# A two-block network in f32: no throwaway passes, decay steps spread over more blocks, and another order of splits and softmax in attention

## The chip, the cores and the metric

One NeuronCore of a Trainium2 chip runs the whole program. The metric is the device time of one execution in microseconds (us). Engines: TensorE (PE; PEld is its weight load), VectorE (DVE), ScalarE (ACT), GpSimd (POOL), SyncE (SP, here the queue that loads weights).

## What is computed

256 tokens of width 2048 go through two layers, batch 1, everything in f32:

```python
# first layer
h = x + gla(rmsnorm(x)) ; h = h + relu(rmsnorm(h) @ w_up)**2 @ w_down ; x = rmsnorm(h) * final_norm
#   gla: q, k, v, r, g = proj; log_a = log_sigmoid(g @ w_gate_up + b) / 16
#        in chunks of 64: cum = cumsum(log_a); k = k * exp(total - cum)
#        state = exp(total) * state + k^T v; o = q @ state; out = (norm(o) * silu(r)) @ w_out
# second layer
h = rmsnorm(x); q, k, v, xr, gr, sc_b, sc_c, sc_x, g_pre = split(h @ w_in)
y_a = softmax(q k^T / sqrt(128) + bias(distance), causal) v @ w_attn_o        # 8 heads of 128
y_b = (gated linear recurrence over conv4(xr)) * gelu(gr) @ w_lru_o
y_c = (sc_b * conv3(sc_c * sc_x)) @ w_sc_o
x = x + (sigmoid(g_a)*y_a + sigmoid(g_b)*y_b + sigmoid(g_c)*y_c) @ w_out
x = x + relu(rmsnorm(x) @ w_up)**2 @ w_down ; out = rmsnorm(x)
```

## The kernel before

**Blocks, units, rounds.** All large products are cut into 236 blocks of 256 output columns each. A block is 4 units (in `mix` 4 or 2) of 512 rows by 256 columns of weights. Weights and activations are split in two fp32r parts, high and low, and a product is two matmuls: high weights against high and low activations (512 columns, L545; L540 where tokens come out) and low weights against high activations (256 columns, L547 or L542). A block of 4 units is 32 such pairs. The order of the blocks is `STREAM`: gk, gv, gq, gr, go, m1 in the first layer; q, k, v, xr, scc, scx, br, scb, mix, lo, m2 in the second. A name with a number is one block: gv5 is the sixth of gv.

**Four slots.** There are 4 slots of raw weights (`raw`) and 4 of split ones (`wsp`); block number r of four units is round r. A unit's way is: SP loads `raw` slot s (L373) as soon as the low split of the last round in this slot is done; ScalarE writes the high part (`split_hi`, L835) as soon as the load has landed and TensorE has used the slot's last unit (`unit_used`); VectorE writes the low part (`split_lo`, L1157); TensorE waits for `lo_done`.

**The order on each engine** is written out by hand and strict. For block i of round r:
- TensorE: `gemm` (4 units, into one of two halves of `acc`), then the block's hooks.
- ScalarE: `evac`: high splits of slots 0, 1, 2 for round r+1, then (block done) the copy of the accumulator's correction part to `corr` (L846), the high split of slot 3, then the hooks.
- VectorE: `take`: low splits of slots 0, 1, 2 for round r+1, the sum `z` (L1167), the block's own elementwise work (for xr: L1188 and two convolutions of 4 taps, L1486 and L1490), `last_split` of slot 3, then the hooks.

**Hooks of the decay stage** (`gla_hooks`, blocks gv0 to gq0). ScalarE has exp and ln of the gate in gv0 (L952, L953); VectorE a subtraction in gv1, the scan of all 2048 columns in gv2 (L1289), the suffix differences and `btot`, `dec` in gv3 (L1293 to L1300), the product with the keys in gv4 (L1304), a softplus in gv5 and gv6; ScalarE exponentiates suffix and `dec` in gv3 (L956, L958). In gv1 to gv7 and gq0 ScalarE also issues one DMA that writes one head's row of position bias 128 times to DRAM (`bias_scratch`, L925).

**Hooks of attention** (`hooks2`, `l2_hooks`; s = 0 to 3 in xr, 4 to 7 in scc, 8 to 11 in scx, 12 in br0). TensorE behind the gemm of block s: q k of head s (L746, L747), transposes of the probabilities of head s-1 (L755, waits for `attn_ready`), probabilities times v of head s-2 (L762, L764), and in s = 4 to 11 a gate product of the recurrence (L776). ScalarE: copy `attnT` (L1058), copy to `hs` (L1061), `weights()`, the exponential of head s (L1050, L1051), and the gates of the recurrence: sigmoid (L1070) and root (L1075) in even s, tanh, exp and square in odd s with `weights()` last. VectorE: logits with scale and bias (L1446, L1448), maximum (L1450, L1451), its negation (L1452), the low part of `hs`, parts of the recurrence, then the normalisation of head s (L1466 to L1468, which waits for the exponential).

**Throwaway passes** (`spacer`, L522): a matmul of 200 columns on data at hand, whose result is overwritten or not read. They stand behind the first pair of the blocks in `BROKEN`, late in the first unit of gr4, one unit behind a norm in mid-block, and in the last six down blocks of m2.

Of the kernel before, what the change touches and what calls it, by code (L numbers as in the profile page):

```python
# [20 lines left out]
P = 128  # L21
T = 256
# [6 lines left out]
SPACE = 200  # L29
# [88 lines left out]
def build(nc, a, out, scratch):  # L118
# [394 lines left out]
    def _(pe):  # L513
        def loop(lo, hi, _):
            return pe.Fori(lo, hi)

        BROKEN = {"gk": (1, 2, 3), "gv": (0, 1), "gq": (0, 2, 3), "gr": (0, 1, 2, 3), "k": (1,), "v": (0,), "xr": range(4),
                  "scc": range(4), "scx": range(4), "br": (0,)}

        def spacer(to):  # L520

            pe.matmul(to[:, 0:SPACE], xs[:, 0, 0, 0:P], xs[:, 0, 0, 0:SPACE], start=True, stop=True, skip_group_check=True)  # L522

        def gemm(b, units, g, x, ready, k0=0, tokens_out=False, mid=None, before=None, mid_unit=2, spaced=False):
# [3 lines left out]
            for u, (rnd, slot) in enumerate(units):  # L528
# [5 lines left out]
                for t in range(UK):  # L534
                    k = UK * u + t
                    start, stop = k == 0, (u == len(units) - 1 and t == UK - 1)
                    for j in range(2):
# [11 lines left out]
                        if spaced is True and u == t == j == 0:  # L549
                            spacer(acc[:, g, 1, 0])  # L550
                        if spaced == "late" and u == 0 and (t, j) == (UK - 1, 0):
                            spacer(flat[1])
                        if mid and u == mid_unit + 1 and (t, j) == (UK - 1, 0):
                            spacer(flat[1])
# [132 lines left out]
        def straight(name, i, b, rnd, g):  # L687
# [3 lines left out]
                 before=before, mid_unit=3, spaced="late" if (name, i) == ("gr", 4) else i in BROKEN.get(name, ()))  # L691
# [12 lines left out]
        def mlp(name, x_base, h_base, norm_no, final):  # L704
# [4 lines left out]
            def down(c, i, b, rnd, g, last=False):  # L709
                gemm(b, units_of(rnd, 0, 4), g, hs, split_upto(h_base + 8 * c), spaced=last and final and not (isinstance(i, int) and i < 2))  # L710
                if last and final:
                    y_transpose(i)
# [67 lines left out]
        def straight2(name, i, b, rnd, g):  # L780
            mid = norm(2, two=True) if (name, i) == ("q", 0) else None
            gemm(b, units_of(rnd, 0, 4), g, xs, split_upto(PAIR0["x2"]), tokens_out=(name == "v"), mid=mid,
                 spaced=i in BROKEN.get(name, ()))
# [32 lines left out]

    def is_past_end(rnd):
        return isinstance(rnd, int) and rnd >= ROUNDS
# [3 lines left out]
    def _(act):  # L822
# [14 lines left out]
        def evac(b, rnd, first, n, g, early=None, late=None):  # L837

            ahead = look_ahead(rnd, first, n)
            for r, s in ahead[:-1]:  # L840
# [75 lines left out]
        def gla_hooks(name, i):  # L916
# [37 lines left out]
            if (name, i) == ("gv", 3):  # L954
# [142 lines left out]
        def second(name, i, b, rnd, g):  # L1097
            if (name, i) == ("q", 0):
                evac(b, rnd, 0, 4, g, early=lambda: std(2), late=second_std)
            else:  # L1100
                evac(b, rnd, 0, 4, g)
# [43 lines left out]
    def _(dve):  # L1145
# [14 lines left out]
        def take(b, rnd, first, n, g, then=None):  # L1160

            for r, s in look_ahead(rnd, first, n)[:-1]:
                split_lo(r, s)
            if then:
# [459 lines left out]
```

## Time and profile before

| | |
|---|---|
| median of 3 runs | 2568.31 us (2568.26 to 2570.51) |
| the profiled execution | 2568.39 us |
| its span, first to last instruction | 2566.6 us |
| granted TensorE clock, mean | 0.997 |
| busy: PE, PEld, DVE, ACT, POOL | 99%, 91%, 71%, 53%, 4% |
| DMA | 504.65 MB, mean 197 GB/s |
| loads of the mlp (512 KB), median to landing | 4.0 and 4.3 us |
| loads of gla_w_in, median to landing | 4.8 us |

The span is what the engines show; the time of an execution lies 1.8 us above it. Durations of matmuls overlap, since they are pipelined: the distance between two starts is what counts. "x3" in a row of the timeline means that three instructions of one kind are merged. In brackets stands how long the engine was idle before, and what ended the wait.

### The profile page before, as it was taken

Reading aid. Unit: us, or ns where it says so; the run is one execution under the profiler, and the core shown is the slowest. Engines: PE = TensorE matmul, PEld = TensorE weight load, DVE = VectorE, ACT = ScalarE, POOL = GpSimd, SP = SyncE. Lnnn points to the kernel's source line nnn. Section 1 sums busy time; section 2 is a strip of 40 time slices with the busy share of each in tenths; the row PEclk is TensorE's granted clock in tenths of the full one; section 3 lists DMA queues with packets and bytes.
Section 4 is the critical chain, followed back from the end, with each engine's and each line's share of the span. In section 5 each row is a group of like instructions: output and inputs, shape, how many; then the busy total and the mean of one; then the engine's idle time right before and its main releaser. Section 6 shows DMA issues by size and latency. Waiting matters only on the chain.

```text
span 2566.6 us, 43594 instructions
## 1 busy us (share of the span) xinstructions
PE 2546.3 (99%) x15628; PEld 2336.8 (91%) x15628; DVE 1815.6 (71%) x2067; ACT 1348.3 (53%) x1635; POOL 95.8 (4%) x96
## 2 busy tenths in 40 slices
PE   9999999999999999999999999999999999999998
PEld 8889999999999999999899999999999999999997
DVE  6767877667666677866897666766777676676675
ACT  6546555444444455544675555555554444454454
POOL 1000020000000002200000000000110000000001
PEclk9999999999999999999999999999999999999999
DMA  7794666666666666775556666666666666666664
GB/s 231 169 207 147 201 202 200 204 199 202 198 197 204 202 198 197 220 216 179 165 173 210 198 202 201 196 196 206 203 198 202 198 196 204 196 202 204 199 200 144
DMA packets 507427, 504.65 MB, mean 197 GB/s; under 512 B 17907, under 2 KB 505608, under 8 KB 507336
## 3 DMA queue, kind: packets, MB, share of 16 engines
q1 hardware_dynamic: 506060, 501.79, 62.6%
q10 hardware_dynamic: 1276, 1.63, 1.5%
q8 instruction: 59, 0.97, 0.2%
q14 instruction: 32, 0.26, 0.0%
HBM read 499.69 MB, written 3.67 MB: 196 GB/s over the span
## 4 chain that ended last, share of the span: by engine, by line
PE 94%; DMA 3%; DVE 2%; ACT 1%; issue 0%; SPq 0%; DVEq 0%; ACTq 0%
PE acc L545 60%; PE acc L547 30%; DMA raw<-in_gla_w_in 3%; PE acc L540 2%; DVE wsp L1157 1%; PE acc L542 1%; DVE lat L1490 0%; ACT wsp L835 0%; DMA xtok<-in_x 0%; PE misc L658 0%; PE misc L673 0%; PE misc L776 0%; PE misc L627 0%; PE misc L675 0%; DVE lat L1486 0%
## 5 line engine op out<-in xcount | busy, mean ns | idle before, releaser
L1157 DVE TENSOR_TENSOR wsp<-raw,wsp 128x1024 fp32r<-128x1024 f32 x944 | 1164.7, 1245 | 491.1 <-ACT wsp L835 456.9
L545 PE MATMUL acc<-xs,wsp 128*128 128x512 f32 x4224 | 1394.0, 383 | 3.5 <-DVE wsp L1157 3.0
L835 ACT ACTIVATE wsp<-raw 128x1024 fp32r<-128x1024 f32 x944 | 991.9, 1058 | 610.2 <-PE acc L547 506.2
L547 PE MATMUL acc<-xs,wsp 128*128 128x256 f32 x4224 | 1151.5, 273 | 0.0
L545 PEld LDWEIGHTS acc<-xs,wsp 128*128 128x128 f32 x4224 | 798.7, 189 | 116.7 <-DVE wsp L1157 5.0
L545 PE MATMUL acc<-hs,wsp 128*128 128x512 f32 x2560 | 841.0, 382 | 0.0
L547 PEld LDWEIGHTS acc<-xs,wsp 128*128 128x128 f32 x4224 | 811.2, 192 | 0.4
L547 PE MATMUL acc<-hs,wsp 128*128 128x256 f32 x2560 | 697.8, 273 | 0.0
L545 PEld LDWEIGHTS acc<-hs,wsp 128*128 128x128 f32 x2560 | 483.9, 189 | 67.2
L547 PEld LDWEIGHTS acc<-hs,wsp 128*128 128x128 f32 x2560 | 491.5, 192 | 0.0
L1167 DVE TENSOR_TENSOR z<-acc,corr 128x512 f32<-128x512 f32 x246 | 200.2, 814 | 184.6 <-ACT corr L846 184.5
L846 ACT ACTIVATE corr<-acc 128x512 f32<-128x512 f32 x246 | 146.9, 597 | 340.5 <-PE acc L547 332.8
L540 PE MATMUL acc<-wsp,xs 128*128 128x512 f32 x384 | 128.1, 386 | 3.8 <-issue 3.8
L486 POOL TENSOR_TENSOR ssq<-ssq,sq 128x256 f32<-128x256 f32 x37 | 30.1, 823 | 2407.4 <-ACT sq L859 1778.8
L542 PE MATMUL acc<-wsp,xs 128*128 128x256 f32 x384 | 105.4, 274 | 0.0
L853 ACT ACTIVATE hs<-z 128x512 f32 (+1 forms) x64 | 40.5, 633 | 99.3 <-DVE z L1385 99.3
L540 PEld LDWEIGHTS acc<-wsp,xs 128*128 128x128 f32 x384 | 73.3, 191 | 15.3 <-issue 5.0
L545 PE MATMUL acc<-mixs,wsp 128*128 128x512 f32 x256 | 83.9, 382 | 0.0
L542 PEld LDWEIGHTS acc<-wsp,xs 128*128 128x128 f32 x384 | 74.5, 194 | 0.0
L547 PE MATMUL acc<-mixs,wsp 128*128 128x256 f32 x256 | 69.8, 273 | 0.0
L1364 DVE TENSOR_TENSOR xres<-xres,z 128x512 f32 (+1 forms) x79 | 54.7, 692 | 12.1 <-DVE z L1167 11.9
L489 POOL TENSOR_TENSOR ssq<-ssq,sq 128x256 f32<-128x256 f32 x37 | 55.9, 1519 | 2.3
(243 smaller groups left out, 1051.6 us busy)
## 6 DMA issues: line engine op xcount, KB each, us to landing
raw<-in_w_in SPq DMA_DIRECT2D x224, 512.0 KB, 4.4
raw<-in_mlp_w_up SPq DMA_DIRECT2D x128, 512.0 KB, 4.0
raw<-in_mlp_w_down SPq DMA_DIRECT2D x128, 512.0 KB, 4.3
raw<-in_w_mlp_up SPq DMA_DIRECT2D x128, 512.0 KB, 4.0
raw<-in_w_mlp_down SPq DMA_DIRECT2D x128, 512.0 KB, 4.3
raw<-in_gla_w_in SPq DMA_DIRECT2D x96, 512.0 KB, 4.8
raw<-in_gla_w_out SPq DMA_DIRECT2D x32, 512.0 KB, 4.5
raw<-in_w_out SPq DMA_DIRECT2D x32, 512.0 KB, 3.8
```

Of the source, the lines that this page charges most:

```text
L486: pool.tensor_tensor(ssq[:, k], ssq[:, k], sq[:, k, 0], ALU.add).then_inc(ssq_half, 1)
L489: ins = pool.tensor_tensor(ssq[:, k], ssq[:, k], sq[:, k, 1], ALU.add)
L540: pe.matmul(both, x[:, k0 + k, 0, cols], taking_turns(both_parts(slot, t)), start=start, stop=False, skip_group_check=True)
L542: ins = pe.matmul(acc[:, g, j, 1], x[:, k0 + k, 1, cols], taking_turns(w_part(0, slot)[:, t]), start=False, stop=stop, skip_group_check=True)
L545: pe.matmul(both, w_part(0, slot)[:, t, cols], taking_turns(x[:, k0 + k]), start=start, stop=False, skip_group_check=True)
L547: ins = pe.matmul(acc[:, g, j, 1], w_part(1, slot)[:, t, cols], taking_turns(x[:, k0 + k, 0]), start=False, stop=stop, skip_group_check=True)
L835: act.activation(w_part(0, slot), raw[:, slot], ACT.Copy).then_inc(hi_done, 1)
L846: act.activation(corr[:, g], acc[:, g, :, 1], ACT.Copy).then_inc(corr_ready, 1)
L853: act.activation(pair(dst, i)[:, :, 0], src[:], ACT.Copy).then_inc(hi_ready, 1)
L1157: dve.tensor_tensor(w_part(1, slot), raw[:, slot], w_part(0, slot).bitcast(F32), ALU.subtract).then_inc(lo_done, 1)
L1167: dve.tensor_tensor(halves(z[:]), in_order(acc[:, g, :, 0]), in_order(corr[:, g]), ALU.add).then_inc(main_read, 1)
L1364: own.done(dve.tensor_tensor(pair(xres, i), pair(xres, i), z[:], ALU.add))
```

## The change

The throwaway passes and the table `BROKEN` go. The scan is made in two halves (gv2, gv3); suffix and `dec` move to gv4, their exponential to gv5, the product with the keys to gv6, the end of the softplus to gv7. In the blocks `PULLED` (xr, scc, scx) both split engines handle slot 0 of round r+2 at the end of block r, ahead of the hooks; the next block then begins with slot 1 (`AHEAD_OF`, `split`). The normalisation of head s leaves the hook of block s for a function of its own, `normalise`, which `take` calls in block s+1 behind the first low split. Scale moves from the logits into q, and logits and maximum become one instruction each for the two parts. The diff, cut to its core; the calls of `spaced` in `down` and `straight2` go in the same way:

```diff
@@ -514,14 +513,7 @@
-        BROKEN = {"gk": (1, 2, 3), "gv": (0, 1), "gq": (0, 2, 3), "gr": (0, 1, 2, 3), "k": (1,), "v": (0,), "xr": range(4),
-                  "scc": range(4), "scx": range(4), "br": (0,)}
-
-        def spacer(to):
-
-            pe.matmul(to[:, 0:SPACE], xs[:, 0, 0, 0:P], xs[:, 0, 0, 0:SPACE], start=True, stop=True, skip_group_check=True)
-
-        def gemm(b, units, g, x, ready, k0=0, tokens_out=False, mid=None, before=None, mid_unit=2, spaced=False):
+        def gemm(b, units, g, x, ready, k0=0, tokens_out=False, mid=None, before=None, mid_unit=2):
@@ -546,12 +538,6 @@
                                             start=False, stop=stop, skip_group_check=True)
-                        if spaced is True and u == t == j == 0:
-                            spacer(acc[:, g, 1, 0])
-                        if spaced == "late" and u == 0 and (t, j) == (UK - 1, 0):
-                            spacer(flat[1])
-                        if mid and u == mid_unit + 1 and (t, j) == (UK - 1, 0):
-                            spacer(flat[1])
                 ins.then_inc(unit_used, 1)
@@ -688,7 +674,7 @@
             gemm(b, units_of(rnd, 0, 4), g, xs, split_upto(PAIR0["x1"]), tokens_out=(name == "gv"), mid=mid,
-                 before=before, mid_unit=3, spaced="late" if (name, i) == ("gr", 4) else i in BROKEN.get(name, ()))
+                 before=before, mid_unit=3)
             hooks(name, i)
@@ -814,6 +799,9 @@
+    PULLED = ("xr", "scc", "scx")
+    AHEAD_OF = [(name, i) for name in PULLED for i in range(4) if (name, i) != ("xr", 0)] + [("br", 0)]
+
@@ -834,10 +822,10 @@
-        def evac(b, rnd, first, n, g, early=None, late=None):
+        def evac(b, rnd, first, n, g, early=None, late=None, split=0):
             ahead = look_ahead(rnd, first, n)
-            for r, s in ahead[:-1]:
+            for r, s in ahead[split:-1]:
                 split_hi(r, s)
@@ -951,7 +939,7 @@
                 act.activation(lat[:], lat[:], ACT.Ln, bias=cst[:, 1:2]).then_inc(gate_ln, 1)
-            if (name, i) == ("gv", 3):
+            if (name, i) == ("gv", 5):
                 act.wait_ge(suffix_done, 1)
@@ -1098,7 +1086,9 @@
             else:
-                evac(b, rnd, 0, 4, g)
+                evac(b, rnd, 0, 4, g, split=(name, i) in AHEAD_OF)
+            if name in PULLED:
+                split_hi(*look_ahead(rnd + 1, 0, 4)[0])
             if name == "br":
@@ -1157,10 +1147,12 @@
-        def take(b, rnd, first, n, g, then=None):
-
-            for r, s in look_ahead(rnd, first, n)[:-1]:
+        def take(b, rnd, first, n, g, then=None, between=None, split=0):
+
+            for k, (r, s) in enumerate(look_ahead(rnd, first, n)[split:-1]):
                 split_lo(r, s)
+                if between and k == 0:
+                    between()
             if then:
@@ -1256,7 +1248,7 @@
                 softplus()
-            if (name, i) == ("gv", 6):
+            if (name, i) == ("gv", 7):
                 softplus_rest()
@@ -1283,11 +1275,12 @@
                 own.done(dve.tensor_tensor(lat[:], mn[:], lat[:], ALU.subtract))
-            if (name, i) == ("gv", 2):
+            if name == "gv" and i in (2, 3):
                 dve.wait_ge(zero_done, 3)
-                fl = [t[:].rearrange("p k t -> p (k t)") for t in (mn, segm, lat)]
+                part = slice((i - 2) * LKT // 2, (i - 1) * LKT // 2)
+                fl = [t[:, part].rearrange("p k t -> p (k t)") for t in (mn, segm, lat)]
                 own.done(dve.tensor_tensor_scan(fl[0], fl[1], fl[2], 0.0, ALU.mult, ALU.add))
-            if (name, i) == ("gv", 3):
+            if (name, i) == ("gv", 4):
                 by = [t[:].rearrange("p k (c s) -> p (k c) s", s=CHUNK) for t in (lat, mn)]
@@ -1299,7 +1292,7 @@
                 ins.then_inc(dec_diff, 1)
-            if (name, i) == ("gv", 4):
+            if (name, i) == ("gv", 6):
                 dve.wait_ge(suffix_exp, 1)
@@ -1443,12 +1436,9 @@
                     dve.wait_ge(at_mm, s)
-                dve.scalar_tensor_tensor(out=attn[:, 0:P], in0=flat[1][:, 0:P], scalar=AD ** -0.5, in1=skew[:, s, P:T],
-                                         op0=ALU.mult, op1=ALU.add)
-                own.done(dve.scalar_tensor_tensor(out=attn[:, P:BW], in0=flat[1][:, P:BW], scalar=AD ** -0.5,
-                                                  in1=skew[:, s], op0=ALU.mult, op1=ALU.add))
-                dve.tensor_reduce(amax[:, 0:1], attn[:, 0:P], AX_X, ALU.max)
-                own.done(dve.tensor_reduce(amax[:, 1:2], attn[:, P:BW], AX_X, ALU.max))
+                dve.tensor_tensor_reduce(attn[:, 0:P], flat[1][:, 0:P], skew[:, s, P:T], 1.0, NEG, ALU.add, ALU.max, amax[:, 0:1])
+                own.done(dve.tensor_tensor_reduce(attn[:, P:BW], flat[1][:, P:BW], skew[:, s], 1.0, NEG, ALU.add, ALU.max,
+                                                  amax[:, 1:2]))
                 dve.tensor_scalar(amax[:], amax[:], -1.0, None, ALU.mult).then_inc(attn_max, 1)
@@ -1461,11 +1451,6 @@
                                                   op1=ALU.mult))
-            if s < AH:
-                dve.wait_ge(attn_exp, s + 1)
-                own.done(dve.reciprocal(ainv[:], asum[:]))
-                dve.tensor_scalar(attn[:, 0:P], attn[:, 0:P], ainv[:, 0:1], None, ALU.mult)
-                dve.tensor_scalar(attn[:, P:BW], attn[:, P:BW], ainv[:, 1:2], None, ALU.mult).then_inc(attn_ready, 1)
             if 6 <= s <= 12 and s % 2 == 0:
@@ -1493,7 +1478,16 @@
+        def normalise(s):
+
+            dve.wait_ge(attn_exp, s + 1)
+            own.done(dve.reciprocal(ainv[:], asum[:]))
+            dve.tensor_scalar(attn[:, 0:P], attn[:, 0:P], ainv[:, 0:1], None, ALU.mult)
+            dve.tensor_scalar(attn[:, P:BW], attn[:, P:BW], ainv[:, 1:2], None, ALU.mult).then_inc(attn_ready, 1)
+
         def second(name, i, b, rnd, g):
+            s = {"xr": 0, "scc": 4, "scx": 8}.get(name, 99) + i
+
@@ -1501,14 +1495,15 @@
-            take(b, rnd, 0, 4, g, first_std if (name, i) == ("q", 0) else None)
+            take(b, rnd, 0, 4, g, first_std if (name, i) == ("q", 0) else None,
+                 between=(lambda: normalise(s - 1)) if 1 <= s <= AH else None, split=(name, i) in AHEAD_OF)
             if (name, i) == ("q", 0):
...
             if name in ("q", "k"):
-                scaled(pair(q2 if name == "q" else k2, i)).then_inc(qkv_ready, 1)
+                scaled(pair(q2 if name == "q" else k2, i), AD ** -0.5 if name == "q" else 1.0).then_inc(qkv_ready, 1)
                 dve.wait_ge(qkv_ready, i + 1 + (4 if name == "k" else 0))
@@ -1548,6 +1543,8 @@
                 emit(PAIR0["yc"] + i, ycs, i)
+            if name in PULLED:
+                split_lo(*look_ahead(rnd + 1, 0, 4)[0])
             l2_hooks(name, i)
```

## Rows read from the trace of the kernel before

**Rows 1.** The page, part 4: the chain that ended last, by engine.
```profile
PE 94%; DMA 3%; DVE 2%; ACT 1%; issue 0%; SPq 0%; DVEq 0%; ACTq 0%
```
**Rows 2.** Timeline of PE in m2: start, us, engine, line, operation, tiles.
```profile
2489.89 0.26 PE L522 MATMUL acc<-xs 128*128 128x200 f32 x1
2489.99 0.40 PE L545 MATMUL acc<-hs,wsp 128*128 128x512 f32 x1
...
2490.33 0.38 PE L545 MATMUL acc<-hs,wsp 128*128 128x512 f32 x1
```
**Rows 3.** Timeline of PE, m1's first block, behind the norm matmuls.
```profile
394.67 0.38 PE L545 MATMUL acc<-xs,wsp 128*128 128x512 f32 x1
...
394.99 0.38 PE L545 MATMUL acc<-xs,wsp 128*128 128x512 f32 x1
```
**Rows 4.** The chain in order of time, 78 to 172: start, us, what.
```profile
97.27 10.58 DMA raw<-in_gla_w_in
...
158.69 8.99 DMA raw<-in_gla_w_in
...
167.70 1.07 ACT wsp L835
...
168.79 1.24 DVE wsp L1157
```
**Rows 5.** DMA view, 95 to 172: issues, KB each, median us to landing.
```profile
bias_scratch<-bias_rows ACTq DMA_DIRECT2D x7, 192.0 KB, 8.8
```
**Rows 6.** Timeline of PE: the first q k matmuls behind four blocks.
```profile
1219.09 0.39 PE L746 MATMUL misc<-k,q 128*128 128x128 f32 x2
...
1232.58 0.39 PE L746 MATMUL misc<-k,q 128*128 128x128 f32 x2
...
1272.25 0.39 PE L746 MATMUL misc<-k,q 128*128 128x128 f32 x2
...
1285.35 0.39 PE L746 MATMUL misc<-k,q 128*128 128x128 f32 x2
```
**Rows 7.** Timeline of DVE, one round in xr.
```profile
1206.21 3.50 DVE L1157 TENSOR_TENSOR wsp<-raw,wsp 128x1024 fp32r<-128x1024 f32 x3 [0.20 <-ACT wsp L835]
...
1216.23 0.28 DVE L1446 SCALAR_TENSOR_TENSOR attn<-misc,skew 128x128 f32<-128x128 f32 x1
...
1216.88 0.29 DVE L1450 TENSOR_REDUCE amax<-attn 128x1 f32<-128x128 f32 x1
...
1217.53 0.17 DVE L1452 TENSOR_SCALAR amax<-amax 128x2 f32<-128x2 f32 x1
1218.75 0.17 DVE L1466 RECIPROCAL ainv<-asum 128x2 f32<-128x2 f32 x1 [1.05 <-ACT attn L1051]
...
1219.70 3.50 DVE L1157 TENSOR_TENSOR wsp<-raw,wsp 128x1024 fp32r<-128x1024 f32 x3 [0.20 <-ACT wsp L835]
```
**Rows 8.** View of line L522: duration ns min/median/max, first and last start.
```profile
L522 PE MATMUL acc<-xs x33: 257/261/268, 24.9 to 2545.0; 128*128 128x200 f32 x33
...
L522 PE MATMUL misc<-xs x4: 258/260/262, 262.5 to 1891.0; 128*128 128x200 f32 x4
```
**Rows 9.** Timeline of DVE, gv2's hook.
```profile
99.77 4.42 DVE L1289 TENSOR_TENSOR_SCAN mn<-segm,lat 128x2048 f32<-128x2048 f32 x1
```
**Rows 10.** Timeline of PE, start of gv5.
```profile
119.33 0.62 PE L540 MATMUL acc<-wsp,xs 128*128 128x512 f32 x1 [3.07 <-issue]
```
**Rows 11.** Windows: busy of the engines, then granted clock, DMA share, GB/s.
```profile
119.30:123.00 3.70, 3.67 (x12) 3.18 (x13) 3.55 (x6) 2.79 (x5) 0.00 (x0) 0.54 0.83 237
```
**Rows 12.** Timeline of ACT, hook of scc2 (s = 6).
```profile
1277.18 0.40 ACT L1050 ACTIVATE attn<-attn,amax 128x128 f32<-128x128 f32 x1 [2.26 <-DVE amax L1452]
...
1278.18 1.28 ACT L1070 ACT_TABLE_LOAD   x1
...
1280.33 1.28 ACT L1075 ACT_TABLE_LOAD   x1
1281.63 0.63 ACT L1075 ACTIVATE lru_u<-lru_t 128x512 f32<-128x512 f32 x1
```

More of the change, by code:

```diff
@@ L28 @@
 SLOTS = 4
-SPACE = 200
 PAIRS = KT // 2
@@ L709, in down @@
             def down(c, i, b, rnd, g, last=False):
-                gemm(b, units_of(rnd, 0, 4), g, hs, split_upto(h_base + 8 * c), spaced=last and final and not (isinstance(i, int) and i < 2))
+                gemm(b, units_of(rnd, 0, 4), g, hs, split_upto(h_base + 8 * c))
                 if last and final:
@@ L781, in straight2 @@
             mid = norm(2, two=True) if (name, i) == ("q", 0) else None
-            gemm(b, units_of(rnd, 0, 4), g, xs, split_upto(PAIR0["x2"]), tokens_out=(name == "v"), mid=mid,
-                 spaced=i in BROKEN.get(name, ()))
+            gemm(b, units_of(rnd, 0, 4), g, xs, split_upto(PAIR0["x2"]), tokens_out=(name == "v"), mid=mid)
             hooks2(name, i)
```

## The prediction

> **What bounds the kernel now.** I read the page first: TensorE is busy for nearly the whole span, and 94% of the chain that ended last is its own [rows 1]. The matmul starts behind a boundary give the beat: a pair (512 and 256 columns) every 0.33 us [rows 2, 3], 32 pairs or 10.48 us a block. So only what breaks that beat can be won, and the two stretches where other things stand in the chain decide.
>
> The first is the decay stage of the first layer (blocks gv1 to gq1). Its chain is a ring: a weight load, its high split, its low split, the next load of that slot. One link is 9.0 to 10.6 us from issue to landing [rows 4], against 4.0 us for the mlp's loads (the table above). The reason stands in the DMA view: each of these blocks also sends a bias broadcast of 192 KB that takes 8.8 us [rows 5]. Link plus two splits is 11.4 to 12.9 us a block, more than 10.48.
>
> The second is attention (xr1 to scx3). The starts of the q k product, the first hook behind each block, stand 13.49 us apart at 1219 to 1232 and 13.10 us at 1272 to 1285 [rows 6]. In the first of these VectorE is a closed ring (1206.21 to 1219.70 [rows 7]) that TensorE waits for; the second is 10.48 plus TensorE's own hooks and spacer, no wait.
>
> **The change, part by part.** *Throwaway passes.* There are 33 and 4 [rows 8]. One costs 0.10 us to the next matmul and 0.01 in the pair behind it (2489.99 to 2490.33 is 0.34) [rows 2]: 0.11 us. Two (gv1, gq0) lie inside the DMA ring and hide; 12 (xr1 to br0) I count in the attention walk; 23 x 0.11 = 2.5 us come off. Does the beat need them? Behind the norm matmuls of m1's first block the pairs run at 0.32 to 0.33 us before any spacer has passed [rows 3]: no. The bound against me is their whole gain, 2.5 us.
>
> *Decays over more blocks.* The 4.42 us scan [rows 9] becomes two of 2.2; the suffix, its exponential and the product with the keys each move a block or more on. Gone should be the 3.07 us hole ahead of gv5 [rows 10], made by ScalarE's high split standing behind an exponential that waited for VectorE, and the half clock behind the hole (0.54 granted over 3.7 us [rows 11]), 1.7 us. Together 4.8. But TensorE's loss here is no sum of holes: the chain of this stage doesn't pass through them, it goes by DMA links to the last wait in gq1. The bias broadcasts stay, one a block, issued behind the same evacuation. What I expect is one link less caught behind a broadcast, because slot 1 no longer loads late: a 10.58 link becomes one of 8.99 [rows 4], 1.5 us. Bounds 0 and 4.8. Softplus, moved beside gq0's splits, costs nothing while that ring is late; without that cover it would be 3 us.
>
> *Logits with maximum in one.* Two elementwise passes and two reductions become two fused passes per head. The reductions take 0.65 us (1216.88 to 1217.53), the passes 0.65 (1216.23 to 1216.88) [rows 7]. The fused one has no row. Nearest is the pass of the same operands: I take 0.65 a head; upper bound 1.30, as if nothing were saved; lower bound 0.5. The Trainium skill ("DVE: opcode table, instruction layouts, handler registers and perf-mode slots", section on datapath and trigger behaviour) says that an accumulation in its own stage has no bubble while the scan runs at half throughput. The scan row (4.42 us for 2048 elements, 2.2 ns each) agrees with its second half; if the fused maximum fell under that half instead, a head would cost about 1.0 us.
>
> *The pulled split and the moved normalisation.* This part sets the sign. In blocks xr, scc, scx ScalarE now makes the high split of the slot 0 two rounds on ahead of its attention work. That split must wait until TensorE has used unit 0 of the **next** block: 2.8 us after the next block has begun (8 pairs, and 0.2 to the release). Queued behind it on ScalarE are the copies of attnT and hs, the exponential, the gates' table loads and functions; before, they ran right behind the evacuation. On VectorE the normalisation of head s-1 leaves its hook and stands in block s behind the low split of slot 1. That needs ScalarE's high split of slot 1, which is issued behind all of ScalarE's hook. TensorE's transposes of that head sit right after gemm s and the q k product, so now they wait for this chain.
>
> I laid the three queues out block by block with the durations of the rows. For before it gives 13.45 where rows 6 have 13.49, and 13.09 where they have 13.10.
>
> xr: before, the ring is 13.49. After: less the reductions (-0.65). From the negated maximum (1217.53) to the next low split were 2.17 us [rows 7]; now 0.2, the exponential 0.9, a high split 1.07 [rows 4] stand there, 2.2 again, and the normalisation (0.8 of the 0.95 between 1218.75 and 1219.70) comes on top behind the split: 13.6. No gain, and in xr1 and xr2 the ring has to be entered first: 13.0 and 14.2 where before has 12.5 and 13.5.
>
> scc3, the worst, counted from the start G of its gemm (head 6): slot-0 unit used G+2.8, high split, low split, fused logits; the exponential starts at G+5.9. Then 0.9, table load 1.28 and sigmoid 0.75 (0.87 to the next load), table load 1.28 and root 0.55 [rows 12], and only then the high split of slot 1, G+10.7; VectorE finishes its scan, splits, normalises: G+14.7. TensorE wanted the result at G+11.1: it waits 3.6 us. Blocks whose ScalarE list has one table load wait 0.7 to 1.5.
>
> The walk's distances between first hooks, from head 0 on: 11.1, 13.0, 14.2, 13.6, 14.4, 13.7, 14.4, 16.6, 14.4, 12.0, 11.3, 11.6, 10.8; sum 171.3. Before: 160.9 by the same walk. That is **+10.4 us**, the 12 spacers already taken off. With a fused pass at 0.5 it is +9.1, at 1.0 +12.7, at 1.30 +14.2. What comes off there are the waits for slots 0 and 3 (3.3 us in all) and the spacers, what comes in are eight waits ahead of the transposes, 14.4 us, and 0.5 us in the br blocks.
>
> Sum against the profiled execution (2568.4, span 2566.6, which stands at the median 2568.3): 2568.4 - 2.5 - 1.5 + 10.4 = 2574.8, so **2575**, 0.26% slower. The measurement can tell some 0.2%, 5.1 us.
>
> **Rivals.** *1, the waits are hidden (faster).* If ScalarE reached the slot-1 split 1.5 us sooner than I count in the odd heads and 3.6 in head 6, no transpose would wait: then -2.5 -1.5 -3.3 (waits removed) -1.3 (12 spacers): 2559.8. For it: in scc3 the exponential starts at 1277.2 [rows 12], 8 us ahead of the next first hook at 1285.35 [rows 6], so today there is slack. Against: both queues are strict in order and the walk meets before's rows within 0.05. It decides from the point where the normalisation ends before G+11.1. *2, half of it (same).* Waits half as long leave +3: 2568, at most 2573. *3, the half clock.* A 3.07 us hole was enough for the lower level, 1.2 GHz, in gv5 [rows 10, 11]; a 3.6 us hole ahead of head 6's transposes may do the same, as I forecast it, 1.6 us: 2576.5. The Trainium skill ("TensorE: Matmul & The Clock Gate", section on HAM oscillation) has the rule that idle between bursts sends the engine back to the lower clock; by it the price is paid, and the trace of gv5 agrees. The rows leave it open, since only one hole of that size is there. *4, the fused pass is dear.* At 1.30 a head: 2578.6; with the half clock 2580. *5, the beat needs the spacers.* Then the 2.5 us don't come: 2577.5.
>
> **How the numbers follow.** Forecast 0.48 (2571 to 2579), rival 1 0.14, 2 0.13, 3 0.13, 4 0.08, 5 0.04. From 2566 to 2581 holds 0.8: out are most of rival 1 and the tail of 4. Slower by over 0.2% (above 2573.4): three quarters of the forecast, 3, 4 and 5, 0.61. Within: the rest of the forecast and most of 2, 0.24. Faster: 0.15. If slower, my own range is 2571 to 2579.
>
> **What would show it.** The starts of L746's matmuls (q k) at distances 13, 14.2, 13.6, 14.4, 13.7, 14.4; TensorE idle ahead of the transposes of heads 0 to 7, longest at head 6, put down to VectorE's normalisation; no wait any more in the third unit of xr2 to scc0; ScalarE's L835 waiting some 4 us for TensorE in scc blocks. Unspaced pairs at 0.33 us. In the decay stage no hole of 3 us and no half clock, but the links of 9 to 10.6 us still there, and gq2 starting at 176 instead of 177.5. Wrong I'd be if the transposes never wait, or if links shrink to 4 us.

## The result and the profile after

The changed kernel takes **2576.7 us** (median of 8 runs, 2573.2 to 2581.3) against 2568.7 (2568.1 to 2570.5) on the same chip: ratio 1.0033, 95% interval 1.0022 to 1.0044. The forecast was 2575. The profiled execution is one of the quickest: 2573.5, span 2571.7, clock 0.998. The changed kernel's runs lie 8.1 us apart and these eight of the other 2.4; in the later comparisons, with 12 to 27 runs, the kernel before spreads over 3.7 to 5.5. The wider spread is a finding of its own (below).

Where the span went, from the starts of the blocks' first pairs in the two traces, after minus before: decay stage (gv1 to gq2) 99.5 against 104.5, **-4.9**; attention (xr0 to br1) 174.3 against 161.1, **+13.2**; all the rest, spacers and 1.0 us of start-up, -3.2; together +5.1. The 1.0 us of start-up differ from profile to profile (see after_dram).

Page, part 4, by engine, where before has 3% DMA [rows 1]; then the waits view of PE and of ACT, 1184 to 1340 (us in all, times, longest):

```profile
PE 95%; DVE 2%; ACT 1%; issue 1%; DMA 0%; SPq 0%; DVEq 0%; ACTq 0%
```
```profile
PE misc L741 <- DVE attn L1486: 13.8, 8, 3.8
...
ACT wsp L823 <- PE acc L539: 43.5, 12, 8.0
```

All of TensorE's waiting in attention is now for the moved normalisation: eight waits, 13.8 us (forecast: eight, 14.4). The high splits (L823) wait for TensorE 12 times; in the scc blocks the pulled one waits 4.4 to 4.5 us (forecast some 4), and the longest wait, 8.0 us, is in scx0, behind head 6. ScalarE's timeline in scc3 has the order that makes it: pulled split, exponential, table load of the root, and only then the high split of slot 1 (the first of x2), which VectorE needs ahead of the normalisation:

```profile
1275.13 1.06 ACT L823 ACTIVATE wsp<-raw 128x1024 fp32r<-128x1024 f32 x1 [4.46 <-PE acc L539]
...
1278.24 0.41 ACT L1038 ACTIVATE attn<-attn,amax 128x128 f32<-128x128 f32 x1 [1.40 <-DVE amax L1442]
...
1281.40 1.28 ACT L1063 ACT_TABLE_LOAD   x1
...
1283.23 1.99 ACT L823 ACTIVATE wsp<-raw 128x1024 fp32r<-128x1024 f32 x2
```

PE's timeline has the q k starts [rows 6], the waits ahead of the transposes, and the first pairs of scx0:

```profile
1212.00 0.39 PE L732 MATMUL misc<-k,q 128*128 128x128 f32 x2
...
1226.15 0.39 PE L732 MATMUL misc<-k,q 128*128 128x128 f32 x2
...
1267.96 0.39 PE L732 MATMUL misc<-k,q 128*128 128x128 f32 x2
...
1270.35 0.55 PE L741 MATMUL misc<-ident,attn 128*128 128x128 f32 x3 [1.56 <-DVE attn L1486]
...
1282.73 0.39 PE L732 MATMUL misc<-k,q 128*128 128x128 f32 x2
1287.33 0.90 PE L741 MATMUL misc<-ident,attn 128*128 128x128 f32 x3 [3.78 <-DVE attn L1486]
...
1290.65 0.99 PE L537 MATMUL acc<-xs,wsp 128*128 128x512 f32 x1
...
1291.65 0.63 PE L537 MATMUL acc<-xs,wsp 128*128 128x512 f32 x1
```

From 1212.00 to 1226.15 are 14.15 us, where [rows 6] have 13.49; from 1267.96 to 1282.73 are 14.77, where before has 13.10. Behind the 3.78 us hole stands the lower clock that [rows 11] showed once before. Windows: length, busy PE, PEld, DVE, ACT, POOL, then **granted clock**, DMA share, GB/s:

```profile
1287.90:1290.65 2.75, 2.75 (x10) 2.30 (x9) 2.68 (x4) 0.00 (x0) 0.00 (x0) 0.50 0.78 224
1290.65:1292.65 2.00, 2.00 (x8) 1.70 (x7) 0.34 (x1) 0.00 (x0) 0.00 (x0) 0.55 0.80 233
```

0.50 is the lower level, 1.2 GHz; the first pairs of scx0 are 1.00 and 0.64 us apart in place of 0.33. The fused logits, DVE's timeline in xr1 [rows 7]: from the first part to the negation 0.67 us, as forecast (0.65).

```profile
1209.85 0.28 DVE L1439 CUSTOM_DVE_ANT_0 attn<-misc,skew 128x128 f32<-128x128 f32 x1
1210.06 0.08 DVE L1439 DVE_READ_ACCUMULATOR2_ANT amax<- 128x1 f32 x1
1210.06 0.42 DVE L1440 CUSTOM_DVE_ANT_0 attn<-misc,skew 128x256 f32<-128x256 f32 x1
1210.40 0.08 DVE L1440 DVE_READ_ACCUMULATOR2_ANT amax<- 128x1 f32 x1
1210.52 0.17 DVE L1442 TENSOR_SCALAR amax<-amax 128x2 f32<-128x2 f32 x1
```

The decay stage, PE's timeline at gv5 [rows 10] and gv6: short holes in place of 3.07, and no half clock behind them.

```profile
114.31 0.45 PE L532 MATMUL acc<-wsp,xs 128*128 128x512 f32 x1 [0.53 <-issue]
...
125.72 0.45 PE L532 MATMUL acc<-wsp,xs 128*128 128x512 f32 x1 [0.69 <-issue]
```

### The profile page after: what moved, and what is told of

The parts are those of the page before. It is cut to its first block, busy times and chain, and to the rows that moved or that the text cites. A ratio compares the mean times of both kernels' runs of the same rounds, so it can differ in the third digit from the quotient of the medians.

```text
span 2571.7 us, 43522 instructions
## 1 busy us (share of the span) xinstructions
PE 2541.1 (99%) x15591; PEld 2330.7 (91%) x15591; DVE 1806.1 (70%) x2068; ACT 1350.9 (53%) x1635; POOL 95.8 (4%) x96
## 4 chain that ended last, share of the span: by engine, by line
PE 95%; DVE 2%; ACT 1%; issue 1%; DMA 0%; SPq 0%; DVEq 0%; ACTq 0%
PE acc L537 59%; PE acc L539 29%; PE acc L532 3%; PE acc L534 2%; DVE wsp L1147 1%; DVE lat L1475 0%; ACT wsp L823 0%; DMA xtok<-in_x 0%; PE misc L762 0%; PE misc L644 0%; PE misc L659 0%; ACT attn L1039 0%; PE misc L613 0%; PE misc L661 0%; PE misc L741 0%
## 5 line engine op out<-in xcount | busy, mean ns | idle before, releaser
L823 ACT ACTIVATE wsp<-raw 128x1024 fp32r<-128x1024 f32 x944 | 993.8, 1059 | 640.2 <-PE acc L539 548.8
L485 POOL TENSOR_TENSOR ssq<-ssq,sq 128x256 f32<-128x256 f32 x37 | 30.1, 823 | 2413.6 <-ACT sq L847 1785.1
```

Of the source, the lines that this page charges most:

```text
L485: pool.tensor_tensor(ssq[:, k], ssq[:, k], sq[:, k, 0], ALU.add).then_inc(ssq_half, 1)
L823: act.activation(w_part(0, slot), raw[:, slot], ACT.Copy).then_inc(hi_done, 1)
```

## The experiments

Twelve kernels. decays_no_bias leaves out the broadcasts of the attention bias: one later transfer writes other data in their place, so its output is not the reference's. Single runs of one kernel differ by up to 10 us, and the intervals of the ratios reach 2 to 4 us to either side, so small parts are read from the profiled execution. "Stage" is the time from the first pair of gv1 to that of gq2, "attention" that from xr0 to br1, both in the profiled execution.

| kernel | median us (lowest to highest, runs) | ratio to before, 95% | stage | attention |
|---|---|---|---|---|
| before (of each comparison) | 2567.3 to 2568.8 | | 104.5 | 161.1 |
| changed | 2576.7 (2573.2 to 2581.3, 8) | 1.0022 to 1.0044 | 99.5 | 174.3 |
| no_spacers | 2565.0 (2561.6 to 2567.0, 11) | 0.9975 to 0.9993 | 105.4 | 160.2 |
| decays_only | 2568.6 (2567.0 to 2570.3, 11) | 0.9991 to 1.0009 | 105.3 | 161.1 |
| order_only | 2586.7 (2585.0 to 2587.1, 5) | 1.0055 to 1.0083 | 104.5 | 179.2 |
| old_order | 2559.1 (2556.8 to 2565.1, 7) | 0.9957 to 0.9979 | 98.9 | 158.3 |
| norm_moved | 2566.7 (2559.2 to 2569.6, 10) | 0.9975 to 0.9995 | 105.5 | 161.5 |
| pull_only | 2563.6 (2559.3 to 2566.2, 10) | 0.9970 to 0.9989 | 99.4 | 159.5 |
| filled_wait | 2575.3 (2572.1 to 2581.0, 10) | 1.0018 to 1.0037 | 105.6 | 172.0 |
| decays_no_bias | 2559.4 (2559.1 to 2562.2, 6) | 0.9952 to 0.9977 | 96.7 | 161.2 |
| bias_dram | 2555.7 (2553.9 to 2556.1, 4) | 0.9937 to 0.9970 | 96.4 | 158.3 |
| bias_one | 2574.8 (2573.2 to 2575.8, 9) | 1.0018 to 1.0038 | 116.0 | 158.2 |
| before_dram | 2560.2 (2559.6 to 2561.6, 6) | 0.9957 to 0.9981 | 96.7 | 161.2 |
| after_dram | 2571.9 (2570.1 to 2574.0, 11) | 1.0003 to 1.0021 | 96.4 | 175.1 |

### The change taken apart

**no_spacers**

```diff
-                        if spaced is True and u == t == j == 0:
-                            spacer(acc[:, g, 1, 0])
# and the other two calls of spacer
```

> The kernel before without its 37 spacers, nothing else touched. The prediction's term (0.11 us for each of the 23 spacers outside attention, and the walk of the queues for those inside, 1.0 us) gives -3.5 us: about 2565.2. The rival in which the beat of the matmuls needs the spacers gives 0 or a loss of up to 1 us, and a wider spread of the runs: the kernel before spreads over 2.4 us, the changed one over 8.1 us, and if the spacers are what keeps the runs together, this kernel spreads like the changed one.

Measured -3.8 us, in attention -0.9: the term holds, the beat doesn't need the spacers. The runs spread over 5.3 us, where before has 3.9 in the same comparison (23 runs). The profiled run is the slowest of the eleven: only 1.4 us come off its span, since its stage is 0.9 longer and its start 0.7 later than in the profile of before. So the -3.8 rests on the medians.

**decays_only**

```diff
-            if (name, i) == ("gv", 2):
+            if name == "gv" and i in (2, 3):     # the scan in two halves, the steps behind it later, as in the change
```

> The kernel before with the decays over more blocks, nothing else touched; spacers, attention order and logits as before. The prediction's term for it was -1.5 us, because the ring of bias broadcasts and weight loads was to stay: about 2567.2. The profile of the changed kernel has 4.9 us less between the first first-half pair of gate round v's second block and that of q's third, so that by it -4.9 us, about 2563.8, is to be seen, with the bias broadcasts about 10.9 us apart in place of 12.1. If the two edits interact (less spacers, shorter chain), something between -1.5 and -4.9.

Measured nothing (-0.2 us), and the stage is 0.8 us longer. Neither the -1.5 nor the -4.9 of the changed kernel's trace comes with this edit alone.

**order_only**

```diff
+            if name in PULLED:
+                split_hi(*look_ahead(rnd + 1, 0, 4)[0])
...
+                if between and k == 0:
+                    between()                    # normalise(s - 1)
```

> The kernel before with the order of the attention blocks changed (first weight split of the next block ahead of the softmax, normalisation moved into the next block), spacers kept, decays and logits as before, logits and their maximum in two operations as before. The walk of the queues gives +14.3 us, about 2583.0; if the clock drops to half behind the longest wait, as in the profile of the changed kernel, 1.6 to 2.8 us more, up to 2586. The rival in which the waits are hidden gives 0. If it is the order that spreads the runs of the changed kernel over 8.1 us, this kernel spreads as far; if it is the absence of spacers, it does not.

+17.8 us, attention +18.0, where the walk had 14.3 and 1.6 to 2.8 for the clock: 0.7 us more than its upper end. The half clock is there (0.50 in scx0's first 2 us), and with the longer logits the waits ahead of the transposes are 17.0 us in place of 13.8. The order is the whole loss. Its five runs agree within 2.1 us, so nothing here says that order spreads them.

**old_order**

```diff
# of the changed kernel, the order alone is undone
-            if name in PULLED:
-                split_hi(*look_ahead(rnd + 1, 0, 4)[0])
...
-                if between and k == 0:
-                    between()
```

> The changed kernel with the order of the attention blocks as before: without the spacers, decays over more blocks, logits with their maximum in one operation. By the walk of the queues attention gives -2.9 us against the kernel before, the spacers outside it -2.5, the decay stage between -1.5 (the prediction's term) and -4.9 (the changed kernel's trace): -6.9 to -10.3 us, 2558.4 to 2561.8. The rival in which the cost of the changed kernel lies in the missing spacers or in the fused operation gives a time at or above that of the kernel before.

-9.7 us; attention 158.3, which is 1.9 less than without spacers alone: the fused logits (1.9 by the walk). This undoes the loss and keeps the rest: the two orders differ by 16.1 us in attention and 17.6 in the medians.

**norm_moved and pull_only**

```diff
# old_order and, norm_moved:
+                 between=(lambda: normalise(s - 1)) if 1 <= s <= AH else None)
# old_order and, pull_only (with AHEAD_OF and VectorE's split_lo as in the change):
+            if name in PULLED:
+                split_hi(*look_ahead(rnd + 1, 0, 4)[0])
```

> The kernel with the old order of the attention blocks (no spacers, decays over more blocks, fused logits), and only the normalisation moved into the next block; the weight split stays behind the softmax. The walk of the queues gives +3.5 us against the old order from the first unit xr0 to br1 (158.3 us there), so 161.8. If the moved normalisation were the whole cost of the order (the old and the new order differ by 16.1 us), it would be 174.

> The kernel with the old order (no spacers, decays over more blocks, fused logits), and only the first weight split of the next block pulled ahead of the softmax; the normalisation stays at its old place. The walk of the queues gives +1.4 us against the old order from xr0 to br1 (158.3 us), so 159.7. If the pulled split were the whole cost of the order it would be 174. By the walk the two moves are dear only together (3.5 + 1.4 against 13.2 for both).

Attention +3.3 and +1.2 against old_order (walk: 3.5 and 1.4), both together +16.1. The waits view of PE over attention, of norm_moved and of pull_only:

```profile
PE misc L749 <- DVE attn L1490: 3.5, 4, 1.1
```
```profile
PE misc L749 <- DVE attn L1467: 1.0, 4, 0.5
```

Each move alone costs little; together they close a loop. The pulled split makes ScalarE's softmax wait for the next block (its slot is free 2.8 us into it), the moved normalisation makes TensorE wait for a split that ScalarE issues behind that softmax.

### The half clock

**filled_wait**

```diff
+                if s == AH - 1:                  # head 6, ahead of the longest wait
+                    for _ in range(14):
+                        pe.matmul(flat[2][:], xs[:, 0, 0, 0:P], xs[:, 0], start=True, stop=True, skip_group_check=True)
                 pe.wait_ge(attn_ready, s)
```

> The changed kernel with 14 throwaway matmuls of 512 columns (3.1 us at the full clock) ahead of TensorE's longest wait, that before the transposes of head 6 (3.78 us in the profile of the changed kernel), so that the engine idles about 0.7 us there in place of 3.8. The output is that of the reference. If half clock behind the wait costs the block scc3 and the block scx0 what the walk does not explain, both together (34.2 us) fall by 2 to 3 us, and the granted clock stays at 1.00 there. If the slow first pairs of scx0 have another cause (weights that are late), it stays at 34.2 or grows. If that half clock also makes the runs of the changed kernel spread over 8 us, they now agree within 3.

PE's timeline, then the windows view, of filled_wait:

```profile
1293.07 0.33 PE L744 MATMUL misc<-ident,attn 128*128 128x128 f32 x1 [0.61 <-DVE attn L1489]
```
```profile
1294.79:1296.80 2.01, 2.01 (x13) 1.85 (x12) 1.91 (x2) 0.00 (x0) 0.00 (x0) 1.00 0.81 258
```

The hole is 0.61 us, the clock stays at 1.00 (2.4 GHz), and scc3 with scx0 takes 31.8 us in place of 34.2: 2.4 us are the half clock's. The spread stayed at 8.9 us: it has another cause.

But the same trace has the lower clock elsewhere, behind a hole of 1.92 us ahead of head 1's transposes (1220.45), where the changed kernel's profile has a like hole (1.82 us) without it. And after_dram (below) has it a second time, behind 2.23 us ahead of head 7 (1303.27), where the changed kernel has 2.22 us without it; its attention is 0.8 us longer (175.1). Windows view of filled_wait, of after_dram, and of the changed kernel behind its 2.22 us:

```profile
1220.80:1224.15 3.35, 3.35 (x13) 2.90 (x12) 3.21 (x6) 0.00 (x0) 0.00 (x0) 0.50 0.81 243
```
```profile
1303.75:1307.15 3.40, 3.40 (x11) 2.74 (x10) 3.26 (x6) 0.00 (x0) 0.00 (x0) 0.50 0.81 241
```
```profile
1304.60:1308.00 3.40, 3.40 (x20) 3.13 (x21) 3.30 (x5) 0.32 (x1) 0.00 (x0) 1.00 0.73 202
```

So the length of a hole alone does not say whether the clock falls: holes of 1.9 to 2.3 us have it in some executions and not in others.

### The two beats of the decay stage

norm_moved and old_order have the same code up to the second layer, yet their stages took 105.5 and 98.9 us. Times fall into two groups as well: of norm_moved's ten, four lie at 2559.2 to 2561.9 and six at 2565.9 to 2569.6, none between. Part of what moves the runs is thus which of two beats, two spacings of the blocks, the stage falls into. The timelines of both, in the block where the order of issue parts (SP issues a load, ACTq the broadcast), first old_order, then norm_moved:

```profile
109.23 0.37 SPq L373 DMA_DIRECT2D raw<-in_gla_w_in  x1
...
109.60 0.49 ACTq L919 DMA_DIRECT2D bias_scratch<-bias_rows  x1
```
```profile
109.99 0.49 ACTq L919 DMA_DIRECT2D bias_scratch<-bias_rows  x1
...
111.04 0.37 SPq L373 DMA_DIRECT2D raw<-in_gla_w_in  x1
```

In old_order the load gets out 0.4 us ahead of the broadcast and lands in 4.3 us; in norm_moved it comes 1.05 us behind it and takes 9.12. From there each kernel keeps its pattern to gq1: broadcasts 10.2 to 11.7 us apart in old_order, 11.5 to 12.8 in norm_moved. The changed kernel's profile has the quick beat, its slowest runs (2580.0 to 2581.3) fit the other; filled_wait, which is the same code up to the second layer, has the slow one in its profile (105.6). The chain of the changed kernel's profile passes through no load at all there (DMA 0% on its page), and its loads take at most 9.5 us; in the slow beat they take up to 10.6.

**decays_no_bias**

```diff
-                act.dma_start(scratch[hd * P * BW:(hd + 1) * P * BW].rearrange("(h p n) -> h p n", h=1, p=P),
-                              bias_rows[hd:hd + 1].unsqueeze(1).to_broadcast([1, P, BW])).then_inc(bias_out, 16)
```

> The kernel before with the decays over more blocks, and with the eight broadcasts of the attention bias left out of the decay stage: one later transfer writes other data in their place, so the attention bias is not that of the reference. If the ring of broadcasts and weight loads sets the stage, all loads land in about 4 us, the holes of the stage go, and from gv1 to gq2 it takes 96 to 97 us in place of 104.5 (before) and 105.3 (decays over more blocks alone): about 2560 to 2561. If the chain of the decays on VectorE sets it, it stays at 104 to 105.

The stage takes 96.7 us, 8.6 less than decays_only. The ring of broadcasts and loads sets it. Loads land in 4.1 us; then, from the view of the whole run, the later transfer, which writes as many bytes to the same place in DRAM but reads all 128 SBUF partitions (last column: median us to landing):

```profile
raw<-in_gla_w_in SPq DMA_DIRECT2D x31, 512.0 KB, 4.1
...
bias_scratch<-ident ACTq DMA_DIRECT2D x1, 1536.0 KB, 10.8
```

**bias_dram and bias_one**

```diff
# bias_dram: once in gv1, then eight copies from DRAM
+                act.dma_start(rows_out, bias_rows[:]).then_inc(bias_out, 16)
...
-                              bias_rows[hd:hd + 1].unsqueeze(1).to_broadcast([1, P, BW])).then_inc(bias_out, 16)
+                              rows_out[hd:hd + 1].unsqueeze(1).to_broadcast([1, P, BW])).then_inc(bias_out, 16)
# bias_one: all in gv1
+                act.dma_start(scratch.rearrange("(h p n) -> h p n", h=AH, p=P),
+                              bias_rows[:].unsqueeze(1).to_broadcast([AH, P, BW])).then_inc(bias_out, 16)
```

> The kernel with the old order (no spacers, decays over more blocks, fused logits), and the bias broadcast differently: the eight rows (12 KB) are written once to DRAM in the block gv1, and the eight broadcasts of gv2 to gq1 copy a row from DRAM to DRAM in place of reading one SBUF partition 128 times. In the old form a packet of a broadcast takes about eleven times as long as one of a weight load (37% of the 16 DMA engines' time for 1152 packets against 48.5% for 16779 in the stage of the kernel before). If it is the 128 reads of one SBUF partition that are dear, loads land in about 4 us, the stage from gv1 to gq2 takes 96 to 98 us in place of 98.9 (the stage's quick beat) or 105.5 (its slow one), the median is 2553 to 2556, and the runs agree within 4 us. If what is dear is the writing of short rows, the broadcasts still take 8.8 us, and the stage goes as before with its two beats: 2557 to 2565.

> The same kernel, with the eight broadcasts made one transfer in the block gv1, which reads eight SBUF partitions. If reads of one partition are what is slow and those of eight partitions go side by side, it takes little more than one of them does now (8.8 us to some 15), loads are late in one block only: the stage 97 to 100 us. If the total work of the DMA engines is the same, it takes eight times 8.8 = 70 us, and the loads of six blocks share the engines with it: stage 104 or more, 2565 or more.

DMA view, 93 to 172, of old_order and of bias_dram (queue: packets, MB, share of 16 engines; q10 carries the broadcasts), [rows 5]:

```profile
q10 hardware_dynamic: 1008, 1.38, 39.4%
...
raw<-in_gla_w_in SPq DMA_DIRECT2D x30, 512.0 KB, 6.4
bias_scratch<-bias_rows ACTq DMA_DIRECT2D x7, 192.0 KB, 8.9
```
```profile
q10 hardware_dynamic: 1152, 1.57, 5.5%
...
raw<-in_gla_w_in SPq DMA_DIRECT2D x29, 512.0 KB, 4.2
```

The same bytes written, from another source, need a seventh of the engines' time, and loads land in 4.2 us: it was the reads of one SBUF partition that were dear, not the short rows. Nor is it the way from SBUF to DRAM as such: the 1536 KB of decays_no_bias, read from 128 partitions (at 384 us, beside loads of the mlp), landed in 10.8 us, little more than 192 KB from one. bias_dram is the best kernel of the study, 11.7 us faster than before, and its four runs agree within 2.2. bias_one misses: for as long as the one transfer runs, loads crawl. PE's timeline, then the DMA view from 79 to 112 and from 85.3 to 115.2, of bias_one:

```profile
109.80 0.79 PE L540 MATMUL acc<-wsp,xs 128*128 128x512 f32 x1 [12.26 <-DVE wsp L1150]
...
117.82 0.64 PE L540 MATMUL acc<-wsp,xs 128*128 128x512 f32 x1 [2.80 <-DVE wsp L1150]
```
```profile
raw<-in_gla_w_in SPq DMA_DIRECT2D x7, 512.0 KB, 24.0
```
```profile
q10 hardware_dynamic: 1032, 1.57, 41.5%
```

gv3 takes 30.1 us; one block pays what eight paid before, and more. Both fit a limit at the source. One broadcast moves 192 KB in 8.8 us, 22 GB/s. The Trainium skill ("SBUF — State Buffer", section on the DMA port swizzle) says that DMA bandwidth follows the number of SBUF ports that the partitions reach, about 27 GB/s each: one partition is one port, and eight neighbouring ones are two, by which bias_one would need some 29 us as an estimate. Its packets run from 85.3 to 115.2 us, 29.8 us, so the trace agrees. A packet of 1536 bytes took 0.55 to 0.77 us out of one partition (medians of the broadcasts of old_order and norm_moved), 0.20 out of eight, 0.065 out of DRAM. The four loads issued from 83.4 to 92.7 us took 24.0 to 29.4 us to land.

**before_dram and after_dram** (the edit of bias_dram in the kernel before and in the changed one)

> The kernel before, only with the bias broadcasts made from DRAM. It tells what the decays over more blocks are worth where no broadcast holds the loads up. If the decays in few long operations cost TensorE nothing by themselves, the stage from gv1 to gq2 takes 96.7 us as in the kernel with decays over more blocks and no bias, in place of 104.5: about 2560.5. If the long scans hold up the weight splits by themselves (a gap of up to 2 us behind each of the two), it takes 98 to 101 us: 2562 to 2565.

> The changed kernel, only with the bias broadcasts made from DRAM. If the two beats of the stage of the broadcasts are what spreads the runs of the changed kernel (2573.2 to 2581.3), the stage takes 96.4 us in place of 99.5, the median is 2570 to 2571.5, and the runs agree within 4 us. If it is the half clock in attention or another thing that spreads them, they still spread over 8 us. Against the same kernel with the old order of attention (2555.7) the new order then costs 15 to 16 us, as in the traces.

before_dram: stage 96.7 (before 104.5), the same as decays_no_bias. So with the broadcasts out of the way the long scans cost TensorE nothing, and the decays over more blocks gain nothing. after_dram: stage 96.4, and the runs spread over 3.9 us in place of 8.1: the two beats made most of the spread. What is left goes with the clock. Of its eleven runs the four with a mean granted clock of 0.998 took 2570.1 to 2570.7 us, the three with 0.997 up to 2572.1, the four with 0.996 2572.5 to 2574.0. One part is the second half clock in attention (above). Another is the start: the first pair of gk1 lies anywhere from 23.0 to 26.3 us in the fourteen profiles, and that goes with the clock between 8 and 17 us. In six profiles it is 1.00 there and gk1 starts at 23.0 to 23.6; in four 0.81, 24.5 to 25.2; in four 0.62, 25.2 to 26.3. That the lower clock makes gk1 late isn't shown by an edit. Windows of the changed kernel, of before and of after_dram:

```profile
8.00:17.00 9.00, 6.81 (x48) 6.26 (x49) 9.00 (x17) 8.76 (x19) 0.00 (x0) 1.00 0.99 300
```
```profile
8.00:17.00 9.00, 7.18 (x43) 6.61 (x44) 9.00 (x17) 8.28 (x18) 0.00 (x0) 0.81 1.02 314
```
```profile
8.00:17.00 9.00, 6.91 (x29) 6.13 (x30) 9.00 (x17) 7.73 (x16) 0.00 (x0) 0.62 1.01 300
```

Against bias_dram the new order costs 16.2 us by the medians, 15.3 if each is taken against the kernel before in its own comparison, 16.8 in attention.

## Why the prediction was right, and where it was not

**Spacers, right.** 3.5 us forecast in all, 3.8 measured; in attention 1.0 and 0.9. Unspaced pairs run at 0.33 us, so rival 5 falls.

**Order of attention, right in place and mechanism, and a fifth too small in size.** The walk gave 13.0, 14.2, 13.6, 14.4, 13.7, 14.4 between the first hooks of xr1 to scc3; measured are 13.05, 14.15, 13.50, 14.37, 13.94, 14.76. (All thirteen distances as printed add up to 171.1 and not 171.3, which is rounding.) The eight waits are there, longest at head 6 (3.78 us, forecast 3.6). +10.4 was forecast, +13.2 came: 2.4 of the 2.8 is rival 3, the half clock behind that hole (priced at 1.6), shown by filled_wait. So what came is the forecast and rival 3 together; with [rows 10, 11], where a hole of 3.07 us had it, it should have stood in the sum. It came behind head 6 in all three profiles with that hole unfilled (the changed kernel, order_only, after_dram). Rivals 1 and 2 fall. The walk was right for the parts too: 3.5 and 1.4 for the moves alone, 3.3 and 1.2 measured.

**Fused logits, right.** 0.65 us a head forecast, 0.67 measured; rival 4 falls.

**Decay stage, the term that failed.** I put down -1.5 us as "one link less caught behind a broadcast, because slot 1 no longer loads late". The profile of the changed kernel has -4.9, this edit alone has nothing, and without the dear broadcasts its worth is nothing as well (96.7 us with it in decays_no_bias, 96.7 without it in before_dram). With this edit the stage has two beats, some 6 us apart (98.9 to 99.5, and 105.3 to 105.6), and by its times the changed kernel falls into either, run by run. My reading of the 3.07 us hole at gv5 was wrong as well: I put it down to a high split behind an exponential that waits for VectorE, but before_dram keeps that exponential and the long scans, and has no hole there (gv3 to gv7 take 10.48 us each). It was the ring. That the links "of 9 to 10.6 us" would stay was right for the slow beat only; in the profile gq2 came at 171.1, not 176, that is 6.3 us ahead of before, 1.4 of them already at gv1. And the 3 us that the moved softplus was to cost without the cover of a late ring don't come: decays_no_bias has no late ring, and gq0 takes 10.59 us there as in before_dram. The ring's cause, the dear broadcast, stood in [rows 5], and I did not ask what it would be worth to cheapen it: 7.8 us of the stage and 8.1 of the median (before_dram), more than any part of the change gained.

**The sum.** That 2576.7 lies so near to 2575 is in part luck: in the quick runs two errors of opposite sign cancel, -3.4 us in the decay stage and +2.8 in attention. The median lies above the profiled 2573.5, most likely because part of the runs have the slow beat and others a later start; only one run of the changed kernel was profiled. What carries the forecast is the order of attention, which the runs show as it was foretold.

**Open.** What tips a run into one beat isn't settled. In the six profiles of kernels with the split scan and the old broadcasts the beat goes with which of two transfers is issued first at 107 to 111 us: the load 0.4 us ahead in the three with the quick beat, 1.05 us behind in the other three. But this is a sign and not the cause, since they differ a block earlier: the load issued 1.0 us behind the broadcast at 95 to 97 us lands in 9.2 to 9.3 us in the first three and in 10.5 to 10.6 in the others, and no row says why. And decays_only, which differs up to there from old_order by its spacers only, never came below 2567.0 us in 11 runs, so it showed no quick beat.

## What to carry to other kernels

Two moves of instructions in strict queues must be costed together: each was worth 1 to 3 us, both 16, since together they made a loop through three engines. A walk of the queues with the trace's durations found this before any run. Add to it the half clock behind a hole as long as one that already shows it, and count it as possible behind shorter ones: here holes of 1.9 and 2.2 us had it in single executions. And where a stage is a ring through DMA transfers, look at what each transfer costs the DMA engines, not only at its bytes: a broadcast read from one SBUF partition held the weight loads up, and the same rows read from DRAM did not. And where runs of one kernel scatter, compare the stages of their profiles and their granted clocks before a median is put down to an edit.

## What the runs showed of the hardware

A broadcast of 192 KB out of one SBUF partition took 8.8 us and such broadcasts, one a block, filled 39% of the 16 DMA engines' time; out of DRAM they filled 5.5%. Eight times the bytes out of 128 partitions landed in 10.8 us, out of 8 partitions they took 29.8. The broadcasts and the loads fell into one of two patterns that then held from 109 us to the end of the stage; what chooses isn't known. Of TensorE's clock: the holes of 3.07 and 3.78 us were followed by the lower level, 1.2 GHz (0.54 over 3.7 us, 0.50 and 0.55 over 4.8 us). So were a hole of 1.92 us in filled_wait and one of 2.23 us in after_dram, but not one of 2.33 us in order_only nor one of 2.22 us in the changed kernel. The Trainium skill ("TensorE: Matmul & The Clock Gate", section on HAM oscillation) says that idle between bursts brings the lower clock back. The traces agree for the two longest holes; for those of 1.9 to 2.3 us they show it in some executions only.
